# Streaming half of the query columns in the levels of a gated recurrence (Trainium2, one core)

## The chip, the cores and the metric

The kernel runs on one core of a Trainium2 chip. The metric is the device time of one execution in microseconds; lower is better. The engines are named as in the profile: PE (TensorE, matrix products; PEld are its weight loads), DVE (VectorE), ACT (ScalarE), POOL (GpSimd) and SP (the queue that issues the transfers). They run side by side and wait for each other on semaphores only.

## The reference, cut to what matters

The whole model is one block with sparse attention and a gated recurrence, followed by two more layers. The change touches only the recurrence, which is this part of the reference (chunks of 64 positions there, 4 heads, 128 channels a head):

```python
f = lb + (1.0 - lb) * jax.nn.sigmoid(f_raw)       # forget gate, one per channel and position
g = jnp.log(f); k = 1.0 - f
bcum = jnp.cumsum(gc, axis=2)
diff = bcum[:, :, :, None, :] - bcum[:, :, None, :, :]
decay = jnp.exp(jnp.where(tri[:, :, None], diff, -jnp.inf))
scores = jnp.sum(qc[:, :, :, None, :] * decay * kc[:, :, None, :, :], axis=-1)
o_intra = jnp.einsum('bhts,bhsv->bhtv', scores, vc)
```

A score of query t against an earlier key s is a product over the channels of q, k and all gates that lie between s and t.

## The kernel before, in words

The kernel has ten stages, one after the other, with a barrier of all engines between them. The fifth, `stage_hgrn`, computes the recurrence for 1024 positions in eight chunks of 128 (`c`), for four heads at once.

The decayed scores of a chunk are built in eight levels, `LEVELS = [0, 1, 2, 4, 8, 16, 32, 64]`. Level 0 is the diagonal. At level m the 128 positions fall into pairs of neighbouring blocks of m positions; the level settles the scores whose key lies in the earlier block of a pair and whose query lies in the later one. After each level the queries of the later blocks are multiplied by the gate product of the earlier block (`Q`, on DVE), and the keys of the earlier blocks by that of the later one (`Kk`, on POOL), so that the next level needs a plain product again. `halves(x, m, c, side)` is the view of the earlier (0) or later (1) blocks of chunk c, 64 of its 128 positions in either case; `masks[:, li, :]` marks the places that level `li` settles.

For every level and chunk, 64 pairs in all, four engines' steps follow each other:

- PE (line 1232): four products, one for each head, of `Kk` (stationary, 128x128) and `Q` (moving, 128 columns) into PSUM bank c. Each is fp32, which the hardware runs as two passes, each with its own weight load and its own matrix instruction: eight passes for a level and chunk. A pass is what one row of the trace counts.
- DVE (L1168): a predicated copy of the bank (4 heads x 128 columns) into `scores`, where the mask is set.
- DVE (L1173 at level 0, L1177 at the others): the growth of `Q`, 512 columns at level 0 and 256 at the others.
- POOL (L1219): the growth of `Kk`, 256 columns, from level 1 on.

PE may start level li of chunk c when `Q` and `Kk` have been grown at the level before for the same chunk (`grown`, `grown_k`). DVE may copy when PE is done with that level and chunk (`products`), and grows `Q` when its own copy is done (`taken`). With eight chunks in eight banks, PE can be up to one level, eight steps, ahead of DVE. Behind the levels PE waits for all 64 copies (`pe.wait_ge(taken, 64)`) and goes on with the transposes and products that carry the state from chunk to chunk (L1238 to L1275).

Of the kernel before, what the change touches and what calls it, by code (L numbers as in the profile page):

```python
# [21 lines left out]
I32 = mybir.dt.int32  # L22
# [3 lines left out]
P = 128  # L26
# [429 lines left out]
def chain(dve, count):  # L456

    def link(instruction):
        dve.wait_ge(count.sem, count.after(instruction))
    return link  # L460
# [606 lines left out]
def stage_hgrn(K):  # L1067
# [5 lines left out]
    nc = K.nc  # L1073
    Kk = K.view(33232, 4096).rearrange("p (h n) -> p h n", h=4)
# [5 lines left out]
    scores = K.view(41424, 4096).rearrange("p (c h t) -> p c h t", c=8, h=4)  # L1080
# [5 lines left out]
    masks = K.view(48072, 1024).rearrange("p (l t) -> p l t", l=8)  # L1086
# [3 lines left out]
    Q = K.feat[:, 0:4, 0:L]  # L1090
# [6 lines left out]
    products, taken = K.sem("level_products"), K.sem("levels_taken")  # L1097
# [9 lines left out]
    def halves(x, m, c, side):  # L1107

        return x[:, :, c * P:(c + 1) * P].rearrange("p h (b s m) -> p h b s m", s=2, m=m)[:, :, :, side, :]
# [6 lines left out]
    with nc.Block() as block:  # L1116

        @block.sync
        def _(sp):
            sp.dma_start(K.dram["index_scores"], K.scores_idx).then_inc(scores_out, 16)  # L1120
            sp.dma_start(masks, K.dram["masks"]).then_inc(loaded, 16)

        @block.vector
        def _(dve):
            link = chain(dve, dve_c)
            v = nc.vector

            raw = K.vec[:, VEC["lb_raw"]:VEC["lb_raw"] + 4]
            link(v.tensor_tensor(lb, raw, raw, ALU.subtract))
            dve.sem_inc(prep, 1)  # L1130
            dve.wait_ge(sm_e, 1)
            link(v.reciprocal(one_lb, e_lb))
            link(v.tensor_tensor(e_lb, e_lb, one_lb, ALU.mult))
            link(v.tensor_tensor(lb, e_lb, e_lb, ALU.subtract))
            link(v.tensor_scalar(one_lb, lb, -1.0, 1.0, ALU.mult, ALU.add))
            for h in range(4):
                last = v.tensor_scalar(f[:, h, :], f[:, h, :], one_lb[:, h:h + 1], lb[:, h:h + 1],
                                       ALU.mult, ALU.add)
            link(last)
            v.tensor_scalar(k_meta, f[:, :, L:E], -1.0, 1.0, ALU.mult, ALU.add)  # L1140
            link(v.tensor_scalar(Kk, f[:, :, 0:L], -1.0, 1.0, ALU.mult, ALU.add))
            dve.sem_inc(prep, 1)

            dve.wait_ge(scores_out, 16)
            for m in (1, 2, 4, 8, 16, 32, 64):
                pairs = tot[m].rearrange("p h (b s) -> p h b s", s=2)
                link(v.tensor_tensor(tot[2 * m], pairs[:, :, :, 0], pairs[:, :, :, 1], ALU.mult))
            dve.sem_inc(prep, 1)

            before = f[:, :, L:E]  # L1150
            for m in (1, 2, 4, 8):
                pairs = before.rearrange("p h (b s) -> p h b s", s=2)
                kv_ = k_meta.rearrange("p h (b s m) -> p h b s m", s=2, m=m)[:, :, :, 0, :]
                link(v.tensor_tensor(kv_, kv_, pairs[:, :, :, 1].unsqueeze(3).broadcast_to((P, 4, 8 // m, m)),
                                     ALU.mult))
                if m < 8:
                    nxt = tot_meta[:, 0:32 // m] if m != 2 else tot_meta[:, 32:48]
                    nxt = nxt.rearrange("p (h b) -> p h b", h=4)
                    link(v.tensor_tensor(nxt, pairs[:, :, :, 0], pairs[:, :, :, 1], ALU.mult))
                    before = nxt  # L1160
            dve.sem_inc(prep, 1)
            link(v.memset(scores, 0.0))
            dve.wait_ge(loaded, 16)
            for li, m in enumerate(LEVELS):
                for c in range(8):
                    n = 8 * li + c
                    dve.wait_ge(products, n + 1)
                    v.copy_predicated(scores[:, c, :, :],  # L1168
                                      masks[:, li, :].bitcast(I32).unsqueeze(1).broadcast_to((P, 4, P)),
                                      K.bank(c).rearrange("p (h t) -> p h t", h=4)).then_inc(taken, 1)  # L1170
                    dve.wait_ge(taken, n + 1)
                    if m == 0:
                        v.tensor_tensor(Q[:, :, c * P:(c + 1) * P], Q[:, :, c * P:(c + 1) * P],  # L1173
                                        f[:, :, c * P:(c + 1) * P], ALU.mult).then_inc(grown, 1)
                    else:
                        q = halves(Q, m, c, 1)
                        v.tensor_tensor(q, q, of_block(m, c, 0), ALU.mult).then_inc(grown, 1)  # L1177
            dve.wait_ge(kt_mm, 1)
            v.tensor_copy(kT[0:META, :, :], K.bank(4)[0:META, :].rearrange("p (h v) -> p h v", h=4))\
                .then_inc(kt_ev, 1)  # L1180
            dve.wait_ge(upd_mm, 1)
            v.tensor_copy(state, K.bank(5).rearrange("p (h v) -> p h v", h=4)).then_inc(upd_ev, 1)
            for c in range(8):
                if c < 7:
                    dve.wait_ge(kt_mm, c + 2)

                    dve.wait_ge(upd_mm, c + 1)
                    v.tensor_copy(kT, K.bank(4).rearrange("p (h v) -> p h v", h=4)).then_inc(kt_ev, 1)
                    dve.wait_ge(upd_mm, c + 2)

                    dve.wait_ge(o_mm, c + 1)
                    dve.wait_ge(upd_ev, c + 1)
                    for h in range(4):
                        last = v.scalar_tensor_tensor(out=state[:, h, :], in0=state[:, h, :],
                                                      scalar=tot[128][:, h, c:c + 1],
                                                      in1=K.bank(5, P, P * h), op0=ALU.mult, op1=ALU.add)
                    last.then_inc(upd_ev, 1)
                dve.wait_ge(squares, c + 1)
                a = c % 2
                link(v.tensor_scalar(rstd[:, a, :], ssq[:, a, :], 1.0 / P, EPS, ALU.mult, ALU.add))  # L1200
                dve.sem_inc(means, 1)
                dve.wait_ge(roots, c + 1)
                link(v.reciprocal(rstd[:, a, :], rstd[:, a, :]))
                if c >= 2:
                    dve.wait_ge(r_mm, c - 1)
                for h in range(4):
                    last = v.tensor_scalar(r_tok[a][:, h, :], K.bank(c % 2, P, P * h), rstd[:, a, h:h + 1], SC,
                                           ALU.mult, ALU.mult)
                last.then_inc(normed, 1)
# [12 lines left out]
        def _(pe):  # L1222
            pe.wait_ge(prep, 2)
            for li, m in enumerate(LEVELS):
                for c in range(8):
                    n = 8 * li + c
                    if li:
                        pe.wait_ge(grown, n - 7)
                    if li > 1:
                        pe.wait_ge(grown_k, n - 15)  # L1230
                    for h in range(4):
                        last = nc.tensor.matmul(K.bank(c, P, P * h), Kk[:, h, c * P:(c + 1) * P],  # L1232
                                                Q[:, h, c * P:(c + 1) * P], start=True, stop=True)
                    last.then_inc(products, 1)
            pe.wait_ge(prep, 4)
            pe.wait_ge(taken, 64)
            for h in range(4):
                last = nc.tensor.transpose(K.bank(4, P, P * h)[0:META, :], k_meta[:, h, :], K.ident)  # L1238
            last.then_inc(kt_mm, 1)
            pe.wait_ge(kt_ev, 1)  # L1240
            for h in range(4):
                last = nc.tensor.matmul(K.bank(5, P, P * h), kT[0:META, h, :], K.vN[0:META, 0, h * P:(h + 1) * P],
                                        start=True, stop=True)
# [3 lines left out]
            for c in range(9):  # L1247
                if c < 7:
                    for h in range(4):
                        last = nc.tensor.transpose(K.bank(4, P, P * h), Kk[:, h, c * P:(c + 1) * P], K.ident)  # L1250
                    last.then_inc(kt_mm, 1)
                if c < 8:
# [4 lines left out]
                    for h in range(4):  # L1257
                        o = K.bank(c % 2, P, P * h)
                        nc.tensor.matmul(o, scores[:, c, h, :], K.vN[:, 1 + c, h * P:(h + 1) * P],
                                         start=True, stop=False)  # L1260
                        last = nc.tensor.matmul(o, Q[:, h, c * P:(c + 1) * P], state[:, h, :],
                                                start=False, stop=True)
                    last.then_inc(o_mm, 1)
                if c < 7:
                    pe.wait_ge(kt_ev, c + 2)
                    for h in range(4):
                        last = nc.tensor.matmul(K.bank(5, P, P * h), kT[:, h, :], K.vN[:, 1 + c, h * P:(h + 1) * P],
                                                start=True, stop=True)
                    last.then_inc(upd_mm, 1)
                if c >= 1:  # L1270
# [3 lines left out]
                    for h in range(4):  # L1274
                        last = nc.tensor.transpose(K.bank(2 + (c - 1) % 2, P, P * h), r_tok[(c - 1) % 2][:, h, :],  # L1275
                                                   K.ident)
# [2159 lines left out]
```

## Time and profile before

| | |
|---|---|
| median of 3 runs | 2954.44 us (2953.98 to 2956.29) |
| profiled execution, its own time | 2952.93 us |
| its span, first to last instruction | 2951.1 us |
| PE busy in the span | 90% |
| DVE busy in the span | 66% |
| mean granted TensorE clock, share of full speed | 0.953 |

The span is the part of the profiled execution that the trace covers; its own time is 1.83 us longer. The median of the runs lies 1.51 us above the profiled execution. The levels take 75 us of the span, from 638.9 us to 713.2 us. The PEclk column of a view is the granted TensorE clock: 1.00 is 2.4 GHz and 0.50 is 1.2 GHz. Matrix instructions overlap, so their durations in a row are longer than the distance from one to the next.

### The profile page before, as it was taken

What the parts mean: (1) busy time and instruction counts of PE and PEld (TensorE: products, weight loads), DVE (VectorE), ACT (ScalarE), POOL (GpSimd) and SP (SyncE); (2) the same over time, 40 slices, a digit from 0 to 9 for tenths busy, and PEclk for the clock granted to TensorE, in tenths of its full rate; (3) what the DMA queues carried; (4) which work ended last, traced back from release to release, by engine and by line L of the source; (5) the groups of instructions that cost most, each with busy time, mean ns of one, the idle gap of its engine ahead of it and who ended that gap; (6) DMA issues with size and microseconds to landing.
All of it is one profiled execution on the core that took longest, in us unless ns stands there. A gap on an engine that the chain in (4) does not pass through costs nothing. (4 is left out here: it accounts for less than half of the span.)

```text
span 2951.1 us, 30727 instructions
## 1 busy us (share of the span) xinstructions
PE 2662.7 (90%) x11185; PEld 1833.4 (62%) x11185; DVE 1943.6 (66%) x3165; ACT 917.9 (31%) x1649; POOL 833.7 (28%) x619
## 2 busy tenths in 40 slices
PE   5999789968599978799999999999999997999967
PEld 1444345457356556577787899987788884444456
DVE  6677369998676578665841777774764425887553
ACT  2121131101344332446434555554432220111132
POOL 0000000023021156676632222116632221233235
PEclk9999899989799989899999999999999998999988
DMA  5122300110100044245746221305321123111043
GB/s 166 61 79 82 130 23 29 36 37 1 57 1 1 1 178 150 67 140 182 274 157 218 79 79 40 86 15 164 122 79 43 44 78 153 47 61 61 29 178 107
DMA packets 101231, 260.78 MB, mean 88 GB/s; under 512 B 9939, under 2 KB 29083, under 8 KB 96480
## 3 DMA queue, kind: packets, MB, share of 16 engines
q1 hardware_dynamic: 101088, 258.90, 26.0%
q8 instruction: 86, 1.41, 0.2%
q14 instruction: 57, 0.47, 0.1%
HBM read 197.91 MB, written 60.96 MB: 88 GB/s over the span
## 5 line engine op out<-in xcount | busy, mean ns | idle before, releaser
L313 PE MATMUL psum<-part,part 128*128 128x512 f32 (+1 forms) x1984 | 765.2, 386 | 60.5 <-POOL part L1688 28.3
L314 PE MATMUL psum<-part,part 128*128 128x512 f32 (+1 forms) x1984 | 743.5, 375 | 0.0
L315 PE MATMUL psum<-part,part 128*128 128x512 f32 (+1 forms) x1984 | 741.3, 374 | 0.0
L1688 POOL TENSOR_TENSOR part<-arena,part 128x512 fp32r<-128x512 f32 (+1 forms) x298 | 428.9, 1449 | 679.3 <-ACT part L1682 678.8
L313 PEld LDWEIGHTS psum<-part,part 128*128 128x128 f32 x1984 | 378.9, 191 | 148.6 <-POOL part L1688 50.2
L314 PEld LDWEIGHTS psum<-part,part 128*128 128x128 f32 x1984 | 379.7, 191 | 70.1 <-issue 2.7
L315 PEld LDWEIGHTS psum<-part,part 128*128 128x128 f32 x1984 | 378.6, 191 | 71.8
L1682 ACT ACTIVATE part<-arena 128x512 fp32r<-128x512 f32 (+1 forms) x298 | 181.7, 620 | 346.8 <-PE psum L315 231.0
L221 PE MATMUL psum<-arena 128*128 128x512 f32 (+1 forms) x672 | 232.8, 506 | 18.0 <-DMA arena<-in_w_f 9.9
L1219 POOL TENSOR_TENSOR arena<-arena 128x256 f32<-128x256 f32 x56 | 39.4, 705 | 666.5 <-PE psum L1232 666.5
L221 PEld LDWEIGHTS psum<-arena 128*128 128x128 f32 x672 | 114.5, 193 | 137.0 <-issue 128.1
L2996 PE MATMUL psum<-arena 128*128 128x512 f32 x448 | 192.9, 592 | 0.0
L1004 DVE TENSOR_SCALAR_CACHE_REDUCE arena<-arena 128x384 bf16<-128x384 f32 (+2 forms) x198 | 173.9, 941 | 1.9 <-PEq L100 0.8
L2518 DVE TENSOR_REDUCE arena<-psum 128x1 f32<-128x1280 f32 x64 | 95.5, 1492 | 103.0 <-PE psum L2470 103.0
L2996 PEld LDWEIGHTS psum<-arena 128*128 128x128 f32 x448 | 85.1, 190 | 107.1 <-issue 107.1
L2982 PE MATMUL psum<-arena 128*128 128x512 f32 x256 | 118.9, 624 | 27.2 <-DVE arena L3083 14.1
L829 PE MATMUL psum<-arena 128*128 128x512 f32 x272 | 125.7, 617 | 16.3 <-DVEq L422 14.1
L2567 ACT ACTIVATE part<-psum 128x512 fp32r<-128x512 f32 (+1 forms) x192 | 93.6, 522 | 146.1 <-PE psum L2479 146.1
L2531 DVE TENSOR_TENSOR part<-psum,part 128x512 fp32r<-128x512 f32 (+1 forms) x192 | 109.1, 596 | 39.4 <-ACT part L2567 39.3
L3011 ACT ACTIVATE arena<-psum 128x512 f32<-128x512 f32 x64 | 36.1, 599 | 301.8 <-POOL arena L3105 174.1
L2806 DVE TENSOR_SCALAR arena<-arena 128x511 f32<-128x511 f32 (+1 forms) x48 | 29.9, 624 | 122.0 <-ACT arena L2785 121.8
L2982 PEld LDWEIGHTS psum<-arena 128*128 128x128 f32 x256 | 50.8, 200 | 94.5 <-issue 81.0
(325 smaller groups left out, 4148.7 us busy)
## 6 DMA issues: line engine op xcount, KB each, us to landing
arena<-in_ada_w SPq DMA_DIRECT2D x24, 1024.0 KB, 6.1
arena<-in_w_hy SPq DMA_DIRECT2D x40, 512.0 KB, 3.3
scratch_spec<-arena SPq DMA_DIRECT2D x68, 256.0 KB, 2.0
arena<-scratch_spec SPq DMA_DIRECT2D x12, 1024.0 KB, 5.2
arena<-in_w_gate SPq DMA_DIRECT2D x16, 512.0 KB, 4.2
arena<-in_w_out SPq DMA_DIRECT2D x16, 512.0 KB, 3.9
arena<-in_w_mgate SPq DMA_DIRECT2D x16, 512.0 KB, 3.5
arena<-in_w_mout SPq DMA_DIRECT2D x16, 512.0 KB, 3.9
```

What stands on the lines that cost most here:

```text
L221: last = nc.tensor.matmul(acc, slot_w[s][:, c], rhs(k, n0, n), start=(k == 0), stop=(k == kt - 1))
L313: nc.tensor.matmul(acc, a_hi, b_hi, start=start, stop=False)
L314: nc.tensor.matmul(acc, a_hi, b_lo, start=False, stop=False)
L315: return nc.tensor.matmul(acc, a_lo, b_hi, start=False, stop=stop)
L829: last = mm(K.bank(4 + n % 2), mats[:, m * P:(m + 1) * P], Y[:, y, :], start=(q == 0), stop=(q == 1))
L1004: last = v.tensor_scalar(junk[:, (block_at(n + 2) - block_at(2)):(block_at(n + 3) - block_at(2))], s, against if isinstance(against, float ...
L1682: self.K.nc.scalar.activation(self.hi[i % 2][:, c], self.raw[i % 2][:, c], ACT.Copy).then_inc(self.rounded, 1)
L1688: self.K.nc.gpsimd.tensor_tensor(self.lo[s][:, c], self.raw[s][:, c], self.hi[s][:, c].bitcast(F32), ALU.subtract).then_inc(self.split, 1)
L2518: v.reduce_max(top[:, i % 2:i % 2 + 1], K.psum[:, at:at + LC], AX_X).then_inc(topped, 1)
L2531: v.tensor_tensor(pT_lo[g % 2][:, k0:k0 + cnt, cols], chunk_bank(n, cnt).rearrange("p (k n) -> p k n", n=P), pT_hi[g % 2][:, k0:k0 + cnt, ...
L2982: last = nc.tensor.matmul(K.bank(4 * (g % 2) + b), fwd[:, m * P:(m + 1) * P], tile(it, PAIRS[n], part), start=(part == 0), stop=(part == 1))
L2996: last = nc.tensor.matmul(K.bank(n), inv[:, m * P:(m + 1) * P], tile(it, r, part), start=(q == 0), stop=(q == len(blocks) - 1))
```

## The change

From level 1 on, PE streams only the 64 query columns of the later blocks of a chunk, gathered by a strided view, and writes them side by side into the first 256 columns of bank c. The predicated copy reads these 256 columns and writes them, with the matching columns of the mask, to the later blocks' places in `scores`. Level 0, the growth of `Q` and `Kk`, the order of all instructions and all waits stay. In the changed kernel the copy of the levels stands at L1173, and the products at L1244.

```diff
                     dve.wait_ge(products, n + 1)
-                    v.copy_predicated(scores[:, c, :, :],
-                                      masks[:, li, :].bitcast(I32).unsqueeze(1).broadcast_to((P, 4, P)),
-                                      K.bank(c).rearrange("p (h t) -> p h t", h=4)).then_inc(taken, 1)
+                    if m == 0:
+                        v.copy_predicated(scores[:, c, :, :],
+                                          masks[:, li, :].bitcast(I32).unsqueeze(1).broadcast_to((P, 4, P)),
+                                          K.bank(c).rearrange("p (h t) -> p h t", h=4)).then_inc(taken, 1)
+                    else:
+                        later = lambda x: x.rearrange("p (b s m) -> p b s m", s=2, m=m)[:, :, 1, :]
+                        v.copy_predicated(scores[:, c, :, :].rearrange("p h (b s m) -> p h b s m", s=2, m=m)[:, :, :, 1, :],
+                                          later(masks[:, li, :].bitcast(I32)).unsqueeze(1)
+                                          .broadcast_to((P, 4, 64 // m, m)),
+                                          K.bank(c, 256).rearrange("p (h b m) -> p h b m", h=4, m=m)).then_inc(taken, 1)
@@
                     for h in range(4):
-                        last = nc.tensor.matmul(K.bank(c, P, P * h), Kk[:, h, c * P:(c + 1) * P],
-                                                Q[:, h, c * P:(c + 1) * P], start=True, stop=True)
+                        if m == 0:
+                            out, q = K.bank(c, P, P * h), Q[:, h, c * P:(c + 1) * P]
+                        else:
+                            out = K.bank(c, 64, 64 * h).rearrange("p (b m) -> p b m", m=m)
+                            q = halves(Q, m, c, 1)[:, h, :, :]
+                        last = nc.tensor.matmul(out, Kk[:, h, c * P:(c + 1) * P], q, start=True, stop=True)
                     last.then_inc(products, 1)
```

## Rows read from the trace of the kernel before

**Rows 1.** Groups by line and shape, 600 to 760 us: busy us, mean ns, idle before.
```profile
L1232 PE MATMUL psum<-arena 128*128 128x128 f32 x512 | 72.8, 295 | 23.3 <-DVEq L1142 17.5 <-DVE arena L1173 5.5
L1168 DVE COPY_PREDICATED arena<-arena,psum 128x512 f32<-128x512 int32 x64 | 46.1, 721 | 0.0
L1219 POOL TENSOR_TENSOR arena<-arena 128x256 f32<-128x256 f32 x56 | 39.4, 705 | 666.5 <-PE psum L1232 666.5
L1177 DVE TENSOR_TENSOR arena<-arena 128x256 f32<-128x256 f32 x56 | 24.7, 441 | 1.9
L1147 DVE TENSOR_TENSOR arena<-arena 128x512 f32<-128x512 f32 x1 | 0.7, 692 | 0.0
L1147 DVE TENSOR_TENSOR arena<-arena 128x256 f32<-128x256 f32 x1 | 0.4, 426 | 0.0
```

**Rows 2.** Timeline of the levels' start and end: start us, us, engine, line, what.
```profile
640.38 1.21 PE L1232 MATMUL psum<-arena 128*128 128x128 f32 x8 [3.97 <-DVE arena L1173]
641.75 5.35 PE L1232 MATMUL psum<-arena 128*128 128x128 f32 x32 [0.15 <-DVE arena L1173]
...
650.64 0.74 DVE L1168 COPY_PREDICATED arena<-arena,psum 128x512 f32<-128x512 int32 x1
...
712.05 0.72 DVE L1168 COPY_PREDICATED arena<-arena,psum 128x512 f32<-128x512 int32 x1
712.80 0.42 DVE L1177 TENSOR_TENSOR arena<-arena 128x256 f32<-128x256 f32 x1
712.88 0.55 PEld L1238 LDWEIGHTS psum<-arena 128*16 128x16 f32 x4 [7.39 <-issue]
712.91 1.01 PE L1238 MATMUL psum<-arena 128*16 128x128 f32 x4 [7.23 <-DVE arena L1168]
```

**Rows 3.** PE's weight loads of the stage before, moving 16 columns a pass.
```profile
468.30 1.76 PEld L221 LDWEIGHTS psum<-arena 128*128 128x128 f32 x15
```

**Rows 4.** L1232 alone, by stretch: PE busy, PEld busy, PEclk, DMA share, GB/s.
```profile
627.20:630.60 3.40, 3.40 (x16) 3.40 (x17) 0.50 0.02 6
631.30:635.30 4.00, 4.00 (x38) 4.00 (x38) 1.00 0.02 4
```

**Rows 5.** All engines by stretch: us, busy of PE, PEld, DVE, ACT, POOL, then PEclk.
```profile
607.20:610.60 3.40, 2.41 (x18) 1.94 (x16) 3.26 (x10) 0.78 (x2) 0.00 (x0) 1.00 0.00 0
610.60:614.00 3.40, 0.00 (x0) 0.00 (x0) 3.37 (x9) 0.00 (x0) 0.00 (x0) 0.51 0.00 0
...
637.90:641.30 3.40, 0.92 (x8) 0.92 (x8) 3.30 (x5) 0.00 (x0) 0.00 (x0) 1.00 0.00 0
641.30:644.70 3.40, 3.25 (x17) 3.00 (x16) 3.33 (x6) 0.00 (x0) 1.64 (x2) 0.51 0.00 0
```

**Rows 6.** The same view later, where the clock stays at 0.50.
```profile
801.80:805.20 3.40, 3.22 (x13) 2.23 (x14) 1.67 (x11) 1.46 (x8) 1.37 (x5) 0.50 0.00 0
805.20:808.60 3.40, 3.22 (x14) 2.23 (x14) 2.17 (x14) 1.46 (x8) 1.41 (x5) 0.50 0.00 0
808.60:812.00 3.40, 3.22 (x14) 2.16 (x14) 2.11 (x12) 1.33 (x6) 1.35 (x5) 0.50 0.00 0
```

**Rows 7.** Timeline there: the weight loads of two passes of 16 columns.
```profile
801.96 0.55 PEld L1584 LDWEIGHTS psum<-arena 128*128 128x128 f32 x2
```

**Rows 8.** Groups by line and shape, 799 to 814 us.
```profile
L1584 PE MATMUL psum<-arena 128*128 128x16 f32 x16 | 3.6, 304 | 0.0
L1584 PEld LDWEIGHTS psum<-arena 128*128 128x128 f32 x16 | 4.4, 333 | 0.0
```

**Rows 9.** All engines by stretch, behind the levels.
```profile
716.00:720.00 4.00, 4.00 (x20) 3.64 (x20) 1.38 (x2) 0.00 (x0) 0.00 (x0) 0.52 0.01 4
720.00:725.00 5.00, 4.07 (x35) 3.64 (x33) 2.68 (x11) 2.81 (x11) 0.00 (x0) 1.00 0.00 0
```

## The prediction

> **What bounds the levels now.** I read the groups of instructions of the stage first, to see which engine has no idle time. DVE's two groups of the levels sat idle for 0.0 and 1.9 us before their 120 instructions, while POOL waited for PE through the stretch (its 666.5 us hold everything since the span's start) [rows 1]. Then the timeline. The copies of levels 1 to 7 start at 650.64 us (the first of 56) and at 712.05 us (the last), so a level and chunk costs DVE (712.05 - 650.64) / 55 = 1.117 us; right behind the last copy, at 712.91, PE leaves its wait and goes on with the state products [rows 2]. So DVE sets the end of the levels. But PE is not far away: it starts level 1 at 640.38, ten microseconds ahead of DVE [rows 2], and must then send eight passes for each level and chunk.
>
> What a pass costs decides this case. By stretches, at full clock PE sends 38 passes in 4.00 us, 0.105 to 0.11 us each; at a granted clock of 0.50 it sends 16 in 3.40 us, 0.2125 us each [rows 4]. The clock is not full all the time here. It falls to 0.50 at about 641.3, behind a stretch in which PE was busy for 0.92 of 3.40 us (it stands idle for 3.97 us while DVE clears the scores and begins level 0 [rows 2]). It is back after one stretch in which PE streamed passes of 128 columns almost back to back, busy 3.25 of 3.40 us [rows 5].
>
> **The change, part by part.**
>
> *The copy.* 56 predicated copies go from 512 to 256 columns; nothing in the trace has this form. The same engine's fp32 product takes 0.692 us at 512 columns and 0.426 at 256, so 0.266 less [rows 1]. The copy at 512 takes 0.721. Bounds: no gain (0.72), or half (0.36). I take 0.721 - 0.266 = 0.455, since the growth, with the same strided halves, takes 0.441 for 256 columns, much like the contiguous 0.426: strides cost little. DVE then needs 1.117 - 0.266 = 0.851 us for a level and chunk. By DVE alone: 56 x 0.266 = 14.9 us gained.
>
> *The products.* 448 passes go from 128 to 64 moving columns. Their weight loads stay, 128x128 each. In the projection before, 15 weight loads that serve passes of only 16 columns take 1.76 us; less the last one's own 0.19 that is 14 steps of 0.112 us at full clock. That is the pace of a pass of 128 columns [rows 3, 4]. So at full clock I cost this half of the change at nothing: the weight load is the floor, PE keeps 8 x 0.112 = 0.90 us for a level and chunk, and its ten microseconds of lead cover the 0.045 us by which it would now be slower than DVE. For the pass itself the bounds are 0.056 (half) and 0.112. The Trainium skill, page "TensorE: Matmul & The Clock Gate", section "Back-to-back issue gap", gives some 60 cycles (an estimate of 25 ns) for matmuls of 1 to 64 columns. By that PE would drop far below DVE, and the sum would stay DVE's 14.9 us; the row with 16 columns speaks against it here.
>
> *The pass at half clock.* Where the clock was 0.50, a pair of weight loads for passes of 16 columns takes 0.55 us, at 0.333 for one load. So the second starts 0.22 us behind the first, although only 16 columns stream between them [rows 7, 8]. That is the pace of a pass of 128 columns at this clock, 0.2125 [rows 4]. So at 1.2 GHz a pass of 64 columns costs 0.2125 too, and eight of them 1.70 us: twice what DVE needs. The same page, section "LDWEIGHTS (loading the stationary operand)", has columns / 1.2 in ns, an estimate of 107 for this load, with no word of the granted clock; by it PE would hold 0.90 us and the gain of 14.9 would stand. The row with 0.22 contradicts it at 1.2 GHz.
>
> *Which clock.* Nothing ahead of level 1 changes, so the idle 3.97 us and the fall at 641.3 stay. While DVE is still at level 0, a PE with half passes has even less to stream. What changes is the way back. Before, the passes at 1.2 GHz carried 128 columns, which fill all of the 0.2125 us (they are the reason for it); PE streamed without a hole and the next stretch was at 2.4 GHz. Now each carries 64 columns: the array streams for half of each step and waits for weights in the other. Do such passes bring the clock back? The nearest rows are 801.8 to 812.0, where pairs of 128 columns alternate with pairs of 16. PE is on record as busy for 3.22 us of each 3.40, and in three stretches running the clock stays at 0.50 [rows 6]. In the other direction, at 607.2 to 610.6, 16 column passes on and off at 2.4 GHz, busy 2.41 of 3.40 us, did not hold the clock [rows 5]. Against: no row has 64 columns in an unbroken row of weight loads. I take it that the clock stays at 1.2 GHz from 641.3 to the end of the levels.
>
> **The sum.** PE's second step of level 1 starts at 641.75, at half clock. From there 55 steps remain of 8 x 0.2125 = 1.70 us: 93.5 us. Its waits cost nothing more, since DVE and POOL (0.851 and 0.705 us a step) follow within the eight steps of slack, and the growth that PE waits for is long done. The last pass goes out at 735.25; some 0.2 us for its tail, 0.455 for the copy and 0.05 between give 735.95. Before, the last copy ended at 712.77 [rows 2]. So the levels end 23.2 us later. Behind them nothing changes: before, PE also began there at half clock, and was at full clock from 720 on [rows 9]; a phase shift may move this by 2 us. The profiled execution would go from its own 2952.93 to 2976.1 us. The median of the runs lies 1.5 us above it: **2977.6 us**. POOL's 0.705 and DVE's 0.851 lie beneath PE's 1.70 and cost nothing; even a copy that stays at 0.721 would change only the last one, 0.27 us.
>
> **Rivals.**
>
> *The clock comes back (faster).* The place is the stretch behind 641.3. If a PE that issues without a pause gets 2.4 GHz back with 64 columns too, and keeps it, DVE bounds the levels and gains 14.9 us: 2954.4 - 14.9 = 2939.5 us. Its cap is PE: 49 steps of 0.90 us behind 650.78 end at 694.9 and the last copy at 695.5, a gain of 17.3 us at most, 2937. For it: PE is busy from 641.75 on, and before the change such a busy stretch brought the clock back [rows 5]. Against it: the three stretches with 3.22 of 3.40 busy [rows 6]. The Trainium skill, same page, section "Why this matters for your kernels", says that a TensorE kept continuously busy reaches the full clock; by this rule the gain of this rival stands. Chance 0.12. If the copy did not get cheaper either, DVE would keep its pace and nothing would move, 2954.4: 0.02 of this.
>
> *The clock changes to and fro.* It returns for some levels, as the blocks grow from 1 to 32 columns and the streams get smoother. Break-even is where 55 steps take the 70.6 us from 641.75 to 712.3, or 1.28 us each; between 0.90 and 1.70 that is at half clock for 48% of the steps. I give this 0.10, between 2940 and 2972 us, most of it slower.
>
> *The change is neutral on PE because weight loads at half clock are not the floor.* Then 64 columns at 1.2 GHz take 0.107 us, PE holds 0.90 us at either clock, and the time is again 2939.5. The pair at 0.22 us [rows 7] is a short series, so I leave 0.02 within the first rival.
>
> **How the numbers follow.** Half clock throughout: 0.78; clock back: 0.12; to and fro: 0.10. Within the first the range is 2972 (the first level still at full clock for some steps) to 2984 (0.1 us lost at each step's semaphore, 56 x 0.1 = 5.6). To leave out no more than 2 in 10 the range reaches down to 2956, into the third case. Less than 0.2% (6 us), which is about what a measurement of this kernel can tell from no change, holds 2948.5 to 2960.3: 0.05. Faster: 0.12 and a little of the third, 0.13. Slower: 0.82.
>
> **What the profile of the changed kernel would show.** The granted clock at 0.50 from about 641 to about 736, and then some; 16 passes of the products in 3.4 us; DVE's copies near 0.455 us, with 0.8 us of idle time before each, put down to PE's products; PE without idle time inside the levels; the state products beginning at about 736. The prediction is wrong if PEclk reads 1.00 behind 645: then the copies follow each other at 0.85 us and the levels end near 698. A pass at half clock in under 0.15 us would make it wrong as well, even with the clock as I say.

## The result, and the profile after

The changed kernel takes 2980.27 us (median of 4 runs, 2974.45 to 2986.10) against 2955.36 us for the kernel before, measured again beside it. The ratio is 1.0084 with a 95% interval of 1.0062 to 1.0106: it is slower, by some 25 us. The profiled execution took 2977.99 us, its span is 2976.2 us.

The groups by line and shape of the changed kernel, 600 to 790 us, answer to [rows 1]. L1244 holds the products, L1226 the growth of keys, L1174 the copies of the levels (the profile has them at this line, not at L1173 as said above), L1184 the growth of queries:

```profile
L1244 PE MATMUL psum<-arena 128*128 128x64 f32 x448 | 95.2, 417 | 4.1 <-DVE arena L1180 4.1
L1226 POOL TENSOR_TENSOR arena<-arena 128x256 f32<-128x256 f32 x56 | 39.8, 710 | 697.0 <-PE psum L1244 697.0
L1174 DVE COPY_PREDICATED arena<-arena,psum 128x256 f32<-128x256 int32 x56 | 28.9, 515 | 28.4 <-PE psum L1244 28.4
L1184 DVE TENSOR_TENSOR arena<-arena 128x256 f32<-128x256 f32 x56 | 28.8, 514 | 1.9
```

The copies are cheaper in sum (56 take 28.9 us, where 64, level 0's eight among them, took 46.1), but DVE now stands idle for 28.4 us ahead of them, and PE is what it waits for. PE's passes carry half the columns and take longer in the rows (417 ns against 295). Why stands in the stretches (us; busy us of PE, PEld, DVE, ACT, POOL; PEclk; DMA), which answer to [rows 5] and [rows 4]:

```profile
637.90:641.30 3.40, 0.26 (x2) 0.27 (x3) 3.33 (x4) 0.00 (x0) 0.00 (x0) 1.00 0.00 0
641.30:644.70 3.40, 3.14 (x19) 3.00 (x19) 3.30 (x6) 0.00 (x0) 1.09 (x2) 0.66 0.00 0
644.70:648.10 3.40, 3.40 (x18) 3.40 (x17) 3.33 (x6) 0.00 (x0) 2.35 (x3) 0.50 0.00 0
...
660.00:680.00 20.00, 20.00 (x95) 20.00 (x95) 16.11 (x32) 0.00 (x0) 9.05 (x12) 0.50 0.00 1
...
700.00:720.00 20.00, 20.00 (x96) 20.00 (x95) 10.52 (x24) 0.00 (x0) 7.31 (x12) 0.50 0.00 1
720.00:736.00 16.00, 16.00 (x77) 16.00 (x76) 8.64 (x19) 0.00 (x0) 5.74 (x10) 0.50 0.01 2
```

The granted clock falls to 0.50 inside 641.3 to 644.7, as before the change, and then stays there to the end of the levels. PE is busy without a gap and sends some 95 passes in 20 us, 0.21 us each; weight loads fill the whole time as well. All four runs show it: their mean granted clock is 0.935 to 0.940, where the profiled execution before had 0.953. Before the change the clock was already back at 645 us (the view of the kernel before):

```profile
645.00:647.00 2.00, 2.00 (x18) 1.89 (x17) 1.93 (x4) 0.00 (x0) 1.91 (x3) 1.00 0.00 0
```

The timeline of the changed kernel, start and end of the levels, answers to [rows 2]:

```profile
641.04 1.11 PE L1244 MATMUL psum<-arena 128*128 128x64 f32 x8 [3.80 <-DVE arena L1180]
642.40 11.99 PE L1244 MATMUL psum<-arena 128*128 128x64 f32 x55 [0.26 <-DVE arena L1180]
...
652.32 0.71 DVE L1174 COPY_PREDICATED arena<-arena,psum 128x256 f32<-128x256 int32 x1
...
734.86 0.45 DVE L1174 COPY_PREDICATED arena<-arena,psum 128x256 f32<-128x256 int32 x1 [0.76 <-PE psum L1244]
734.90 0.62 POOL L1226 TENSOR_TENSOR arena<-arena 128x256 f32<-128x256 f32 x1 [1.09 <-PE psum L1244]
...
736.57 0.44 DVE L1174 COPY_PREDICATED arena<-arena,psum 128x256 f32<-128x256 int32 x1 [0.76 <-PE psum L1244]
...
737.15 1.01 PE L1249 MATMUL psum<-arena 128*16 128x128 f32 x4 [0.63 <-DVE arena L1174]
```

The copies of the last two steps start 1.71 us apart (734.86 and 736.57), each after 0.76 us of waiting for PE, and PE begins the state products at 737.15 where it began at 712.91 before: 24.2 us later, nearly the whole of the 25.1 us by which the span grew. Part of the rest is the way back behind the levels: in 744 to 748 us the clock is at 0.90, so it was low until about 744.8, 7.7 us behind the start of the state products, where [rows 9] with 0.52 in 716 to 720 give 6.9. Both are estimates from the means of a stretch.

### The profile page after: what moved, and what is told of

Read it like the earlier page. It is cut to its first block and busy times, and to the rows that moved or that the text cites. A ratio compares the mean times of both kernels' runs of the same rounds, so it can differ in the third digit from the quotient of the medians.

```text
span 2976.2 us, 30727 instructions
## 1 busy us (share of the span) xinstructions
PE 2692.5 (90%) x11185; PEld 1872.4 (63%) x11185; DVE 1939.6 (65%) x3165; ACT 918.2 (31%) x1649; POOL 832.7 (28%) x619
## 5 line engine op out<-in xcount | busy, mean ns | idle before, releaser
L1226 POOL TENSOR_TENSOR arena<-arena 128x256 f32<-128x256 f32 x56 | 39.8, 710 | 697.0 <-PE psum L1244 697.0
L221 PEld LDWEIGHTS psum<-arena 128*128 128x128 f32 x672 | 114.0, 193 | 136.0 <-issue 127.4
L3007 PEld LDWEIGHTS psum<-arena 128*128 128x128 f32 x448 | 85.1, 190 | 107.1 <-issue 107.1
L1244 PE MATMUL psum<-arena 128*128 128x64 f32 (+1 forms) x512 | 104.7, 405 | 23.0 <-DVEq L1142 18.9
L1244 PEld LDWEIGHTS psum<-arena 128*128 128x128 f32 x512 | 104.2, 319 | 23.4 <-DVEq L1142 19.0
```

The lines of the kernel that those rows point to most:

```text
L221: last = nc.tensor.matmul(acc, slot_w[s][:, c], rhs(k, n0, n), start=(k == 0), stop=(k == kt - 1))
L1244: last = nc.tensor.matmul(out, Kk[:, h, c * P:(c + 1) * P], q, start=True, stop=True)
L3007: last = nc.tensor.matmul(K.bank(n), inv[:, m * P:(m + 1) * P], tile(it, r, part), start=(q == 0), stop=(q == len(blocks) - 1))
```

## The experiments

Each is told with its edit against the changed kernel, unless it says otherwise. Ratios are to the kernel before, whose runs on the same chip were made beside them.

### e1: the copies alone

```diff
-                                          K.bank(c, 256).rearrange("p (h b m) -> p h b m", h=4, m=m)).then_inc(taken, 1)
+                                          K.bank(c).rearrange("p (h b s m) -> p h b s m", h=4, s=2, m=m)[:, :, :, 1, :]).then_inc(taken, 1)
...
-                        if m == 0:
+                        if True:
                             out, q = K.bank(c, P, P * h), Q[:, h, c * P:(c + 1) * P]
```

> Half of the change alone: PE streams all 128 query columns again; only the predicated copy takes 256 columns (read with strides from the bank). Theory (the granted clock falls to 1.2 GHz behind 641 us and passes of 64 columns never bring it back; the copy itself is a gain): PEclk is 1.00 from about 645 us on, a copy takes 0.44 to 0.52 us, DVE needs about 0.85 us a level and chunk, the levels end near 698 us and the time is some 15 us below before, about 2940 us. Rival (the strided copy, and the growth beside it, cost DVE more than they save): DVE's step stays at 1.1 us or more and the time is 2954 or above.

2954.14 us, ratio 0.9997 (0.9987 to 1.0006): no change. The loss is gone with the narrow passes, but the expected gain of 15 us is not there. The copies did get cheaper. Groups of e1, 660 to 690 us:

```profile
L1184 DVE TENSOR_TENSOR arena<-arena 128x256 f32<-128x256 f32 x28 | 18.5, 661 | 1.0
L1226 POOL TENSOR_TENSOR arena<-arena 128x256 f32<-128x256 f32 x28 | 18.1, 648 | 13.0 <-PE psum L1244 13.0
L1174 DVE COPY_PREDICATED arena<-arena,psum 128x256 f32<-128x256 int32 x28 | 13.8, 494 | 0.0
```

In a stretch as long (27 to 28 steps) the kernel before gave the growth of queries 442 ns; here it takes 661. What the copy saves, the growth gives back. Only the last steps keep the gain: POOL's last growth ends at 704.64 us, from then on DVE's growths take 0.42 us and its steps 0.81, and PE waits 5.53 us there for the last copy, where it waited 7.23 us before [rows 2]. The timeline of e1 shows how the rest is lost:

```profile
678.58 2.03 PEld L1244 LDWEIGHTS psum<-arena 128*128 128x128 f32 x16 [0.18 <-DVE arena L1184]
678.68 0.63 POOL L1226 TENSOR_TENSOR arena<-arena 128x256 f32<-128x256 f32 x1 [0.43 <-PE psum L1244]
678.90 0.69 DVE L1184 TENSOR_TENSOR arena<-arena 128x256 f32<-128x256 f32 x1
679.51 0.42 DVE L1174 COPY_PREDICATED arena<-arena,psum 128x256 f32<-128x256 int32 x1
679.82 0.63 POOL L1226 TENSOR_TENSOR arena<-arena 128x256 f32<-128x256 f32 x1 [0.51 <-PE psum L1244]
679.96 0.77 DVE L1184 TENSOR_TENSOR arena<-arena 128x256 f32<-128x256 f32 x1
680.66 0.42 DVE L1174 COPY_PREDICATED arena<-arena,psum 128x256 f32<-128x256 int32 x1
680.79 0.30 PEld L1244 LDWEIGHTS psum<-arena 128*128 128x128 f32 x2 [0.17 <-DVE arena L1184]
```

The growth of queries ends 0.28 us behind POOL's growth of keys each time: 679.31 and 679.59, 680.45 and 680.73. It was so before the change too, with nothing to see in the durations: POOL's growth of 692.57 us ends at 693.19, DVE's of 693.05 at 693.47. From this I infer a ring: PE's release at 678.58, POOL's start at 679.82 when that step's products are done (1.24), POOL's end (0.63), the held growth's end (0.28), and PE's next release at 680.79. (PE may start a step when the queries of the step eight before it have grown; counted through the trace, the growth of a step is held up by POOL's work for the sixth step behind it, and two steps are left between the two.) The ring takes 2.2 us and carries two steps, 1.10 us each, which is also what DVE's own work took before the change. The Trainium skill, page "SBUF — State Buffer", section "SBUF: two separate sides", says that a DVE operation with two SBUF inputs and a GpSimd operation that reads SBUF lock each other out of a shared port pair for the whole instruction. The trace agrees: the held growth ends 0.28 us behind POOL's instruction each time, however long its own row is.

### e2: the products alone

```diff
-                    if m == 0:
+                    if True:
                         v.copy_predicated(scores[:, c, :, :],
...
-                            out = K.bank(c, 64, 64 * h).rearrange("p (b m) -> p b m", m=m)
+                            out = K.bank(c, P, P * h).rearrange("p (b s m) -> p b s m", s=2, m=m)[:, :, 1, :]
```

> The other half alone: PE streams 64 columns from level 1 on, and writes them with strides to their old places in the bank; the copy takes 512 columns as before. Theory: the clock stays at 1.2 GHz from about 641 to 736 us, a pass costs 0.213 us, PE sets the step of 1.70 us, and the copy of 0.72 us hides beneath it: the levels end 0.3 us later than with the whole change, and the time is the changed kernel's, 2975 to 2986 us. Rival (DVE's new copy is the cause): the time falls back to before's, 2955 us.

2978.65 us, ratio 1.0072 (1.0053 to 1.0090). One stretch of e2 and its copies, of 512 columns again:

```profile
680.00:700.00 20.00, 20.00 (x95) 20.00 (x95) 13.42 (x24) 0.00 (x0) 7.69 (x12) 0.50 0.00 1
```

```profile
L1169 DVE COPY_PREDICATED arena<-arena,psum 128x512 f32<-128x512 int32 x64 | 46.5, 726 | 18.3 <-PE psum L1244 18.3
```

The narrow passes alone make the whole loss, as expected, and a copy of 0.73 us hides beneath PE's step.

### e3, e10, e11: level 1 with 128 columns, the rest with 64

```diff
-                        if m == 0:
+                        if m <= 1:
                             out, q = K.bank(c, P, P * h), Q[:, h, c * P:(c + 1) * P]
```

The copy of level 1 reads the bank as in e1.

> The whole change, but level 1 still streams 128 columns; levels 2 to 7 stream 64. It asks whether the loss is in how the clock comes back, or in passes of 64 columns as such. If only the way back is barred, PEclk goes to 1.00 near 645 us with level 1 and stays there: a pass of 64 columns then follows the last one in 0.112 us, DVE sets the step, and the time is about 2941 us. If passes of 64 columns with DVE's pace do not hold the full clock either, it falls again within level 2 and does not return: some 48 steps at 1.70 us, about 2968 to 2975 us. I put 60 on the first and 40 on the second. Rival (a strided pass of 64 columns is slow by its own access, whatever the clock): 0.21 us a pass while PEclk reads 1.00.

2965.27 us is the median of ten runs from 2948.00 to 2979.85; the ratio is 1.0039 (1.0014 to 1.0064). They fall into two groups. Five lie at 2948.00 to 2958.74 us, with a mean granted clock of 0.949 to 0.954; five lie at 2971.80 to 2979.85 us, with 0.939 to 0.942. The trace of e3 is of the fastest. e10 and e11 are the same kernel, profiled twice more.

> e3 once more, for its trace: its ten runs spread from 2948 to 2980 us. Theory: in the long ones the clock was lost in a level with 64 columns and did not come back; a run near 2950 shows PEclk at 1.00 to the end of the levels, a run above 2965 shows 0.50 from some point on, with steps of 1.70 us behind it.

> e3 a third time, for its trace, with the same two outcomes as e10: PEclk at 1.00 to the end and a time near 2950 us, or 0.50 from some point of the levels on, steps of 1.70 us behind it and a time above 2965 us.

These took 2973.13 and 2980.97 us. Three traces of one program, by stretches, e3 first:

```profile
648.10:660.00 11.90, 10.79 (x79) 9.43 (x79) 11.56 (x21) 0.00 (x0) 7.85 (x10) 1.00 0.00 1
660.00:680.00 20.00, 19.89 (x148) 17.66 (x147) 19.39 (x37) 0.00 (x0) 12.03 (x19) 1.00 0.00 1
```

e10:

```profile
644.70:648.10 3.40, 3.02 (x24) 2.53 (x22) 3.30 (x7) 0.00 (x0) 2.12 (x4) 1.00 0.00 0
648.10:652.00 3.90, 3.81 (x24) 3.54 (x24) 3.80 (x7) 0.00 (x0) 2.13 (x3) 0.77 0.00 2
652.00:656.00 4.00, 4.00 (x20) 4.00 (x20) 3.86 (x8) 0.00 (x0) 1.63 (x3) 0.50 0.00 0
...
680.00:700.00 20.00, 20.00 (x96) 20.00 (x95) 10.79 (x24) 0.00 (x0) 7.35 (x12) 0.50 0.00 1
```

e11:

```profile
652.00:656.00 4.00, 3.57 (x28) 3.08 (x27) 3.89 (x7) 0.00 (x0) 2.50 (x4) 1.00 0.00 0
656.00:660.00 4.00, 3.94 (x23) 3.67 (x23) 3.90 (x8) 0.00 (x0) 2.03 (x3) 0.69 0.01 2
660.00:680.00 20.00, 20.00 (x95) 20.00 (x96) 17.27 (x35) 0.00 (x0) 8.61 (x13) 0.50 0.00 1
```

In e3 level 1 brought the clock back, and 48 steps of 64-column passes kept it. In e10 and e11 level 1 brought it back as well, and it fell within level 2, with the same instructions running. Once down it stayed down, with steps of 1.70 us. From PE's first pass of level 1 to the state products e3 takes 69.5 us, e10 and e11 92.7 us each; what else lies between e10 and e11 comes from ahead of the levels, which begin at 635.39 and 642.40 us. So passes of 64 columns at DVE's pace kept 2.4 GHz in one execution and lost it in two, and at 1.2 GHz, with weight loads of 128 columns, they won it back in none of the traces. What decided between the executions stays open.

### e4: weight loads of 64 columns

```diff
-                            out = K.bank(c, 64, 64 * h).rearrange("p (b m) -> p b m", m=m)
+                            out = K.bank(c, 64, 64 * h)[0:64].rearrange("p (b m) -> p b m", m=m)
...
-                        last = nc.tensor.matmul(out, Kk[:, h, c * P:(c + 1) * P], q, start=True, stop=True)
+                        last = nc.tensor.matmul(out, Kk[:, h, c * P:c * P + (P if m == 0 else 64)], q, start=True, stop=True)
```

> As the changed kernel, but from level 1 on the weight loads take 64 columns instead of 128, so that the products of keys 64 to 127 of each chunk are left out (the copy still reads all partitions of the bank). It tests the weight load as the floor. Theory: a pass of 64 columns at 1.2 GHz now costs about 0.107 us instead of 0.213, the array streams without a hole while it is behind, so the clock is back at 1.00 soon behind 645 us at the latest, DVE bounds the levels at about 0.85 us a step and the time is near 2940 us. At the full clock PE has much idle time, so the clock may fall again; even then eight passes at 0.107 are 0.86 us and the time stays below 2945. Rival (64 moving columns are slow by themselves): passes stay at 0.21 us and the time at 2977.

This kernel leaves out half of the scores, those of keys 64 to 127 of each chunk. 2943.06 us, ratio 0.9956 (0.9940 to 0.9973). Its weight loads, eight to a step, first while the clock was at 0.50 (it was there until about 657 us: 652 to 656 reads 0.50, 656 to 660 reads 0.85), then at 1.00:

```profile
641.75 0.93 PEld L1244 LDWEIGHTS psum<-arena 128*64 128x64 f32 x8 [0.46 <-DVE arena L1180]
...
676.24 0.54 PEld L1244 LDWEIGHTS psum<-arena 128*64 128x64 f32 x8 [0.26 <-DVE arena L1184]
...
677.16 0.54 PEld L1244 LDWEIGHTS psum<-arena 128*64 128x64 f32 x8 [0.38 <-DVE arena L1184]
...
677.92 0.63 POOL L1226 TENSOR_TENSOR arena<-arena 128x256 f32<-128x256 f32 x1 [0.29 <-PE psum L1244]
...
678.88 0.54 PEld L1244 LDWEIGHTS psum<-arena 128*64 128x64 f32 x8 [0.38 <-DVE arena L1184]
```

Eight passes of the same 64 moving columns take 0.93 us at 1.2 GHz where the changed kernel needs 1.71. So the moving columns were not what made a pass long: it was the weight load (the edit halves the columns of the array in use along with it, and no run parts the two), and at 2.4 GHz too, where eight loads of 64 columns take 0.54 us and eight of 128 take 0.97 (e3, at 652.34 us). The clock came back here, though some 12 us later than I expected. And with PE at 0.54 us a step, the steps are 0.86 us: the two released starts at 676.24 and 677.16 lie 0.92 us apart, and the next, at 677.96, another 0.80. That is e1's ring again: 0.76 us from PE's release at 677.16 to POOL's start at 677.92, 0.63 for POOL, 0.28 for the growth that it holds up, and 0.05 to PE's release at 678.88 are 1.72 us for two steps.

### e5: POOL grows the keys of two heads of four

```diff
-                    nc.gpsimd.tensor_tensor(k, k, of_block(m, c, 1), ALU.mult).then_inc(grown_k, 1)
+                    nc.gpsimd.tensor_tensor(k[:, 0:2], k[:, 0:2], of_block(m, c, 1)[:, 0:2], ALU.mult).then_inc(grown_k, 1)
```

The edit is against e1. The keys of the other two heads stay ungrown.

> As e1 (128 columns streamed, copies of 256), but POOL grows the keys of two heads of four only (the other two are left ungrown). It asks why e1 gained nothing although its copies took 0.42 us from block size 4 on. Theory from e1's trace: DVE's growth of the queries ends 0.28 us after POOL's instruction in every step, so the two do not run side by side, and a ring of PE (1.24 us from its release to POOL's start), POOL (0.63) and the rest of the growth (0.28) with a wait of 0.05 turns once in two steps: 2.20 / 2 = 1.10 us. With POOL at some 0.33 us the ring would take 0.95 us a step, and PE's own eight passes 0.90. So steps of 0.93 to 0.97 us from block size 4 on, growth back near 0.45 to 0.6 us, and the time 5 to 8 us below before. Rival (PE's step is the bound in e1, by something besides its 0.90 us of passes): steps stay at 1.10 us.

2942.60 us, ratio 0.9963 (0.9948 to 0.9977), below e1, whose instructions on DVE and PE are the same. The timeline of e5:

```profile
689.73 0.40 POOL L1226 TENSOR_TENSOR arena<-arena 128x128 f32<-128x128 f32 x1 [0.49 <-PE psum L1244]
689.82 2.40 PE L1244 MATMUL psum<-arena 128*128 128x128 f32 x20
...
689.91 0.50 DVE L1184 TENSOR_TENSOR arena<-arena 128x256 f32<-128x256 f32 x1
...
690.62 0.40 POOL L1226 TENSOR_TENSOR arena<-arena 128x128 f32<-128x128 f32 x1 [0.49 <-PE psum L1244]
```

Growth again ends 0.28 us behind POOL (690.41 and 690.13). The step is 0.89 us, eight passes of 0.112, PE's own limit at full clock. A shorter growth of keys made PE and DVE faster, so POOL's work was part of what held e1's step at 1.10 us, and PE's passes alone were not. But the step came out below the 0.93 to 0.97 us that I expected: with POOL at 0.40, e1's ring would be 1.24 + 0.40 + 0.28 + 0.05 = 1.97 us for two steps, 0.99 each. The ring did not stay as it was. Counted through the trace, from block size 8 on a growth is now held up by POOL's work for the fifth step behind it, not the sixth, so three steps fit into the 1.97 us, and PE never waits.

### e6: two heads of four with 128 columns

```diff
-                        if True:
+                        if m == 0 or h < 2:
                             out, q = K.bank(c, P, P * h), Q[:, h, c * P:(c + 1) * P]
```

Against e1; heads 2 and 3 write their 64 columns with strides, as in e2.

> As e1, but heads 2 and 3 of every level from 1 on stream 64 columns, heads 0 and 1 stream 128; the copy is e1's. It has half of the narrow passes of the changed kernel. Theory (the loss is the clock that does not come back under passes that are all narrow): with half of the passes full the clock is back at 1.00 within one or two stretches behind 641 us, and the time is e1's and before's, 2950 to 2958 us. Rival (narrow passes cost something of their own): half of the loss stays, some 12 us above before, 2967.

2949.99 us, ratio 0.9984 (0.9975 to 0.9993). By stretches:

```profile
641.30:644.70 3.40, 3.39 (x16) 3.39 (x17) 3.30 (x6) 0.00 (x0) 2.15 (x2) 0.52 0.00 0
644.70:648.10 3.40, 3.40 (x18) 3.40 (x18) 3.33 (x6) 0.00 (x0) 1.92 (x3) 0.50 0.00 0
648.10:660.00 11.90, 11.10 (x85) 9.99 (x85) 11.59 (x20) 0.00 (x0) 8.62 (x11) 0.99 0.00 1
```

With half of the passes full, the clock is back two stretches behind the fall, and 224 narrow passes cost nothing. The kernel before was back after one stretch, so with fewer full passes the way back was longer in this trace. The rival (narrow passes cost something of their own, 2967 us) falls.

### e7, e8, e9, e12: can the smaller copy be made to pay?

e7 is e1 with one line in POOL's loop. e8 is e7, and e9 is e7 with -5 in the place of -6, and both also move the clearing of the scores from DVE to POOL, ahead of the levels; e12 is the kernel before with this move alone.

```diff
-            link(v.memset(scores, 0.0))
+            dve.wait_ge(cleared, 1)
...
+            pool.wait_ge(scores_out, 16)
+            nc.gpsimd.memset(scores, 0.0).then_inc(cleared, 1)
...
                     pool.wait_ge(products, 8 * (li + 1) + c + 1)
+                    pool.wait_ge(grown, 8 * (li + 1) + c - 6)
```

> As e1, with one wait more: POOL starts a growth of keys only when DVE has finished the growth of queries of seven steps earlier, which puts it beside DVE's copy instead of beside its next growth. If DVE and POOL exclude each other in the growths, a step becomes 0.05 + POOL's 0.62 + the 0.28 by which the growth ends later, 0.95 us, with PE's 0.90 beneath it: steps of 0.95 to 1.0 us from block size 4 on, and a time 4 to 7 us below before. If the placing of POOL's work does not matter, 1.10 us and no change.

> As e7, and the scores are cleared by POOL ahead of the levels instead of by DVE between the products of level 0 and their copies. DVE's 3.5 us leave the path, and PE's idle time ahead of level 1 shrinks from 4 us to about 1. Expected: e7's time less 2.5 to 3.5 us, 7 to 10 us below before. If POOL's clearing takes longer than DVE's preparation leaves it (DVE starts the levels at about 635.4 us), up to 2 us of it are lost again.

> As e8, with POOL's extra wait one growth of queries later (six steps behind PE instead of seven). In e7 and e8 that wait was already met when POOL came to it, so their steps stayed at 1.10 us. Now POOL's growth of keys can start only when the growth of queries that it used to hold up is done: it runs beside DVE's copy (0.42 us) and holds up the next growth by the 0.2 us that it lasts longer. Expected from block size 4 on: 0.04 + 0.62 + 0.28 = 0.94 us a step against 1.10, 40 steps, 6 us less than e8, about 2940 us; levels 1 and 2, whose copies take 0.71 us, stay near 1.1. If the exclusion is no cause, the steps stay at 1.10 us; if the later start of POOL holds up PE instead, they grow.

> The kernel before with one thing changed: POOL clears the scores ahead of the levels, as in e8 and e9; products and copies are those of before. It tells how much of e8's 0.33% comes from the clearing and how much from the copies of 256 columns. By the traces of e7 and e8, whose steps were 1.10 us alike and like before's, all of it is the clearing and the idle time that it takes from PE: a ratio to before of 0.996 to 0.999, steps of 1.10 us, growth at 0.43 to 0.44 us and copies at 0.72. If the smaller copies did give something after all, the ratio is above 0.9985.

| kernel | median us | ratio to before | 95% interval |
|---|---|---|---|
| e7 | 2950.18 | 0.9987 | 0.9977 to 0.9996 |
| e8 | 2945.71 | 0.9967 | 0.9955 to 0.9979 |
| e9 | 2946.97 | 0.9972 | 0.9961 to 0.9983 |
| e12 | 2948.46 | 0.9985 | 0.9970 to 0.9999 |

e7's wait was met already when POOL came to it: its copies start at 680.43 and 681.58 us and its growths still take 0.69 and 0.77 us, just as in e1. That expectation was off by one step in the ring. Its time is 0.13% below before all the same, like e6's; 1.7 us of this are the shorter wait behind PE's last pass, as in e1, and the rest is not explained. e9's wait works. Its timeline:

```profile
690.27 0.43 DVE L1175 COPY_PREDICATED arena<-arena,psum 128x256 f32<-128x256 int32 x1
690.49 0.62 POOL L1230 TENSOR_TENSOR arena<-arena 128x256 f32<-128x256 f32 x1 [0.43 <-DVE arena L1185]
690.73 0.66 DVE L1185 TENSOR_TENSOR arena<-arena 128x256 f32<-128x256 f32 x1
691.31 0.43 DVE L1175 COPY_PREDICATED arena<-arena,psum 128x256 f32<-128x256 int32 x1
691.53 0.62 POOL L1230 TENSOR_TENSOR arena<-arena 128x256 f32<-128x256 f32 x1 [0.42 <-DVE arena L1185]
```

The step is 1.04 us instead of 1.10: POOL's 0.62, the 0.28 behind it, and 0.14 from the growth's end (691.39) to POOL's start, where I had expected 0.04. That gives 0.06 us for each of some 40 steps, 2 us, which the runs don't resolve. e8 lies some 10 us below the kernel before (0.9967). e12 shows that the clearing alone gives a good part of this, 0.9985, with copies and products as before. Whether the smaller copies add anything to it stays open, since the intervals of e8 and e12 overlap.

e12 also shows what the fall of the clock hangs on. PE's wait ahead of level 1 is 0.21 us there instead of 3.97, and the clock does not fall in the levels at all, as in e8 and e9:

```profile
641.30:644.70 3.40, 2.69 (x19) 2.12 (x19) 3.33 (x6) 0.00 (x0) 2.03 (x3) 1.00 0.00 0
```

The changed kernel with this move was not run. Whether it would keep the full clock is open, since e10 and e11 lost it without such a wait.

## Why the prediction was right, step by step

**The clock falls behind 641 us and does not come back: right.** It was the likeliest case, and the trace has PEclk at 0.50 from inside 641.3 to 644.7 to the end of the levels. e2 shows that the narrow passes alone do it, e6 that the same passes do no harm when others between them carry 128 columns, e4 that they don't keep the clock down when the weight loads shrink with them. The reason given, that TensorE streams for half of a step and waits for weights in the other, fits e4's rows: 64 columns with a load of 64 pass in half of the 0.213 us. That the 128 moving columns were the reason for 0.2125 us before is not shown, since the loads alone take as long [rows 7]. PE was busy without a gap from 642.40 us on and the clock stayed down, so being busy was not enough, which was the case for the first rival. The rows that the forecast leaned on were weaker than it took them to be: at 801.8 us PE is busy for 3.22 of 3.40 us only, and at 607.2 us the clock falls in the next stretch, in which PE does nothing [rows 5]. For this kernel four runs of four bore the choice out; one level away it went either way (e3). Before, the step of 1.10 us had 8 x 0.112 us of PE in it and the way back at 1.2 GHz led over full passes; this way was what the change took away.

**A pass of 64 columns costs as much as one of 128: right.** From 642.40 on 440 passes end with the start of the last at about 736.1: 0.213 us each, where the forecast had 0.2125. e4 shows that the weight load of 128 columns is the reason. The Trainium skill, page "TensorE: Matmul & The Clock Gate", section "LDWEIGHTS (loading the stationary operand)", gives columns / 1.2, an estimate of 107 ns for this load. The traces have 112 ns at 2.4 GHz, near it, and 213 ns at 1.2 GHz, twice it; there the measurement decides.

**The sum: right in size.** Forecast 23.2 us for the levels, measured 24.2, of which 0.65 come from PE's second step starting at 642.40 instead of 641.75. The time came out at 2980.27 against 2977.6 us.

**The copy at 0.455 us: right for blocks of 4 and more (0.43 to 0.44), wrong for 1 and 2.** There it stayed at 0.71, the row at 652.32 for 256 columns as [rows 1] for 512. With PE as the bound this cost nothing. Why it is so was not tried.

**"So DVE sets the end of the levels": only half of it.** DVE had no idle time, and its 0.72 and 0.43 us made up the step. But the ring of PE, POOL and the growth that POOL holds up turned at 1.10 us too. In e1 DVE had 0.3 us less of its own work from block size 4 on, and the steps stayed at 1.10 us. So the first rival, with the clock back, was mispriced: from PE's first pass of level 1 to the state products e1 takes 70.8 us and the kernel before 72.5, so of the 14.9 us there were 1.7. With the clock up and 64 columns, e3's faster five runs are at 2948 to 2959 us, not at 2939.5.

**"To and fro" as a case of 0.10:** not this kernel, but one level away from it (e3, e10, e11).

## What to carry to other kernels

Halving the moving columns of fp32 matmuls saves nothing on TensorE where the weight load is already as long as the stream, and it can cost twice: look, before it, for a stretch in which the granted clock falls and must be won back by just those instructions, and for the wait of TensorE ahead of it, since e12 removed the fall by removing the wait. An engine without idle time need not be the only bound: look whether some instruction's end keeps a fixed distance to another engine's, since time saved elsewhere on it will be spent there. Where a kernel's runs spread far more than its neighbour's, take several traces before one is believed.

## What the runs showed of the hardware that was not expected

- The DVE growth (two SBUF inputs) ends some 0.28 us behind POOL's overlapping instruction where POOL's started first, in every trace that was read for it; its row stretches from 0.43 to 0.77 us in e1, and to 1.04 us in level 1 of the changed kernel. Where DVE's starts first, it is POOL's row that stretches, to 1.01 us (0.74 at 659.81, in the same level):

```profile
658.09 0.43 DVE L1184 TENSOR_TENSOR arena<-arena 128x256 f32<-128x256 f32 x1
658.10 1.01 POOL L1226 TENSOR_TENSOR arena<-arena 128x256 f32<-128x256 f32 x1 [0.97 <-PE psum L1244]
```

- A predicated copy of 256 fp32 columns takes 0.71 to 0.72 us when its runs are of 1 or 2 elements, and 0.42 to 0.44 us with runs of 4 and more; the growth of queries on the same halves took 0.43 us at block size 1 where POOL did not hold it (658.09 us in the changed kernel).
- With identical instructions the granted clock was held at 2.4 GHz through 48 steps of 64-column passes in one execution (e3) and fell in their first eight in two others (e10, e11).
- Weight loads of 128x128 fp32 follow each other in 0.112 us at 2.4 GHz and 0.213 at 1.2; of 64 columns, eight take 0.54 and 0.93 us.
